# The last weight unit in sixteen transfers of eight partitions instead of one of 128

## The reference

```python
def moe_swiglu(h, w_router, w_gate, w_up, w_down):
    logits = (h @ w_router).astype(jnp.float32)
    top_vals, top_idx = lax.top_k(logits, TOP_K)
    top_w = jax.nn.softmax(top_vals, axis=-1)
    combine = jnp.sum(jax.nn.one_hot(top_idx, N_EXPERTS, dtype=jnp.float32) * top_w[..., None], axis=-2)
    y = jnp.zeros_like(h)
    for e in range(N_EXPERTS):
        y = y + combine[..., e:e + 1] * swiglu(h, w_gate[e], w_up[e], w_down[e])
    return y
# x = x + moe_swiglu(rms_norm(x, g_ffn_norm), ...); return rms_norm(x, g_final)
```

## Time and profile before

| | |
|---|---|
| median of 3 runs | 1340.99 us |
| lowest and highest | 1340.85 and 1341.76 us |
| the profiled execution's own time | 1340.35 us |
| its span, from the first to the last instruction | 1338.6 us |
| mean granted clock of TensorE, share of full speed | 0.998 |
| mean rate of the DMA engines over the span | 332 GB/s |

### The profile page before, as it was taken

How to read it: one execution, slowest core, us unless ns; L and a number is a source line. 1 busy time by engine, 2 the same in 40 slices (tenths; PEclk the granted TensorE clock), 3 DMA queues, 4 the chain that set the end, 5 groups by cost and what they waited for, 6 DMA issues and landing times.

```text
span 1338.6 us, 20750 instructions
## 1 busy us (share of the span) xinstructions
PE 1315.4 (98%) x8608; PEld 712.9 (53%) x8608; DVE 677.1 (51%) x1352; ACT 458.1 (34%) x773; POOL 3.6 (0%) x9
## 2 busy tenths in 40 slices
PE   9999999999999999999999999999999999999977
PEld 8887888888888778333333333333333333333322
DVE  5768765554767775444333553342533443433533
ACT  6565554443556554312121212112212112112112
POOL 0000000000000000000000000000000000000000
PEclk9999999999999999999999999999999999999999
DMA  9743555545575369999999999999999999999995
GB/s 350 272 142 99 188 186 189 189 157 160 187 259 188 111 252 364 394 426 426 426 428 426 426 429 425 427 427 427 427 424 429 426 426 429 426 427 426 428 426 207
DMA packets 68387, 444.46 MB, mean 332 GB/s; under 512 B 4632, under 2 KB 10280, under 8 KB 46656
## 3 DMA queue, kind: packets, MB, share of 16 engines
q1 hardware_dynamic: 66688, 440.36, 81.7%
q10 hardware_dynamic: 1296, 2.12, 0.6%
q0 software_dynamic: 304, 0.60, 0.1%
HBM read 442.01 MB, written 1.05 MB: 331 GB/s over the span
## 4 chain that ended last, share of the span: by engine, by line
PE 85%; DMA 6%; DVE 4%; ACT 2%; issue 1%; SPq 0%; DVEq 0%; ACTq 0%
PE A L543 22%; PE A L538 11%; PE DN L543 11%; PE A L532 7%; PE A L534 7%; PE A L533 7%; DMA pair<-in_moe_w_in 6%; PE DN L538 5%; PE T L2196 2%; PE DN L534 2%; PE DN L532 2%; PE DN L533 2%; DMA xs<-in_x 1%; PE A L1957 1%; PE T L534 1%
## 5 line engine op out<-in xcount | busy, mean ns | idle before, releaser
L543 PE MATMUL A<-pair,heTf 128*32 128x512 f32 x2688 | 295.3, 592 | 0.0
L507 DVE TENSOR_TENSOR parts<-raw,parts 128x2048 fp32r<-128x2048 f32 (+3 forms) x83 | 180.0, 2174 | 97.7 <-ACT parts L500 97.6
L538 PE MATMUL A<-pair,heTf 128*64 128x512 f32 x448 | 199.3, 594 | 7.1 <-DMA pair<-in_moe_w_in 7.1
L539 PE MATMUL A<-pair,heTf 128*64 128x512 f32 x448 | 199.4, 594 | 0.0
L543 PEld LDWEIGHTS A<-pair,heTf 128*32 128x32 f32 x2688 | 86.1, 110 | 197.4 <-issue 197.4
L500 ACT ACTIVATE parts<-raw 128x2048 fp32r<-128x2048 f32 (+3 forms) x83 | 150.9, 1821 | 106.3 <-PE A L534 56.4
L1649 DVE STREAM_TRANSPOSE aTf<-one_av 32x128 f32<-32x128 f32 x560 | 169.1, 302 | 12.9
L532 PE MATMUL A<-parts,hTh 128*128 128x512 f32 (+2 forms) x432 | 167.7, 388 | 0.8 <-DVE parts L507 0.6
L533 PE MATMUL A<-parts,hTh 128*128 128x512 f32 (+2 forms) x432 | 163.6, 379 | 0.0
L534 PE MATMUL A<-parts,hTl 128*128 128x512 f32 (+2 forms) x432 | 163.6, 379 | 0.0
L543 PE MATMUL DN<-pair,aTf 128*32 128x512 f32 x1344 | 149.5, 593 | 0.0
(11 more groups left out here) (355 smaller groups left out, 1422.5 us busy)
## 6 DMA issues: line engine op xcount, KB each, us to landing
pair<-in_moe_w_in SPq DMA_DIRECT2D x112, 2048.0 KB, 33.7
pair<-in_moe_w_down SPq DMA_DIRECT2D x55, 2048.0 KB, 33.5
raw<-in_w_in SPq DMA_DIRECT2D x22, 1024.0 KB, 6.0
raw<-in_dense_w_down SPq DMA_DIRECT2D x11, 1024.0 KB, 5.0
raw<-in_dense_w_gate SPq DMA_DIRECT2D x10, 1024.0 KB, 5.1
raw<-in_dense_w_up SPq DMA_DIRECT2D x10, 1024.0 KB, 5.1
raw<-in_w_out SPq DMA_DIRECT2D x8, 1024.0 KB, 5.3
raw<-in_w_br_mla SPq DMA_DIRECT2D x4, 1024.0 KB, 5.1
```

The source lines that it names most:

```text
L507: nc.vector.tensor_tensor(lo[:, :n], raw_of(u)[:, :n], hi[:, :n].bitcast(F32), ALU.subtract).then_inc(lo_done, 1)
L538: nc.tensor.matmul(o[:SMALL], even, w_even, start=start, stop=stop)
L539: return nc.tensor.matmul(o[SMALL:], odd, w_odd, start=start, stop=stop)
L543: return nc.tensor.matmul(o[at * QUARTER:(at + 1) * QUARTER], tokens, w, start=start, stop=stop, tile_position=(0, at * QUARTER))
```

## The change

The last unit is no longer issued as one transfer. A loop over the partitions issues sixteen, each for eight neighbouring partitions with 8 KB each. All add 16 to the same semaphore, so the count that PE waits for goes from 16 to 16 * 16 = 256. Source, destination, place in the issue order and everything else stay as they are.

```diff
             if u == LAST_UNIT:
-                return 16
+                return 16 * (P // 8)
...
                     sp.dma_start(pairs[pair][:, 0, :], src[:, :UNIT]).then_inc(pair_landed[pair], 16)
-                    sp.dma_start(pairs[pair][:, 1, :], src[:, UNIT:]).then_inc(last_landed, 16)
+                    for p in range(0, P, 8):
+                        sp.dma_start(pairs[pair][p:p + 8, 1, :], src[p:p + 8, UNIT:]).then_inc(last_landed, 16)
```

## The result

The changed kernel takes 1344.0 us (median of 14 runs, 1343.56 to 1344.73) against 1340.9 us for the kernel before on the same chip (14 runs, 1340.53 to 1341.76): a ratio of 1.0022, 95% interval 1.0014 to 1.0029. That is +3.1 us, with an interval of 1.9 to 3.9. The profiled execution has 1343.88 us and a span of 1342.1 us (before 1340.35 and 1338.6); its granted clock is 0.998.

What follows compares the result with a forecast made beforehand. The end was taken to hang on a weight pair landed at 1309.00, then compute, leaving the last unit 2.1 us of slack. Profiled 1340.35 + 3.0 = 1343.35 us, stated as 1344.0 against the median; range 1340.8 to 1348.9.

Steps and rivals of the forecast that it cites:

- What bounds the end, and the slack: At the end, the last unit's landing is off the chain, with 2.1 us of slack before PE needs it.
- Packets: In the last unit's transfers, eight engines carry sixteen rows each: 4.95 us in place of 2.47.
- Rival D: One engine carries all rows of the last unit: 39.6 us, +35 us, 1376; chance 0.01.
- Issue: Fifteen more issues on SP, 0.51 us each unhindered or 3.89 if held; taken as no cost, +1.3 us at worst.
- Completions: In the small transfers each engine posts one after every row, not every eighth; taken as nothing, 7.5 us at most.
- Rival C: Each completion of the small transfers is waited out: +8.0 us, 1349.0; chance 0.04.
- Where these rows start: A laggard engine starts the last unit's rows at 1321.2; at full pace PE starts 0.5 us later.
- wrong if the chain up to 1324 moves: The prediction's own failure sign: nothing in its sum touches the chain before PE takes the last activations.
- The pace of these rows: Neighbouring partitions slow the last unit's rows by a factor of 1.5: 7.4 us, landing 1328.6, PE +3.0 us.
- A: Rival, hidden: eight engines at full pace on the last unit, +0.5 us, 1341.5; chance 0.33.
- B: Rival, in step: four engines share one's pace on the last unit, 19.8 us, PE +15.3 us, 1356.3; chance 0.04.
- Chances: For the whole kernel: slower 0.46, within 0.2% (2.7 us) 0.51, faster 0.03; the forecast itself 0.55.

Runs made afterwards that it cites:

- e9: e1 with the rows for partitions 64 and up written to the lower half of another buffer; 1341.02 us, ratio 1.0003.
- e2: Changed kernel with eight transfers of 16 neighbouring partitions in place of sixteen of eight; 1341.79 us, ratio 1.0006.
- e3: Changed kernel, but SP waits until the last pair's first half has landed before issuing the sixteen transfers; 1351.66 us, ratio 1.0080.
- e1: Changed kernel with each of the sixteen transfers taking eight partitions four apart; 1342.97 us, ratio 1.0016.
- e8: e1 with partitions 64 to 127 first and 0 to 63 after; 1343.95 us, ratio 1.0022.
- e6: e3 with weights read from rows four apart, still written into neighbouring partitions; 1350.61 us, ratio 1.0072.
- e4: e3 with the eight partitions of each transfer four apart, read and written; 1353.98 us, ratio 1.0097.
- e7: e3 with neighbouring weight rows read into partitions four apart; 1353.76 us in its only run.

## Why the prediction was right or wrong

*What bounds the end, and the slack.* Right. The sum from the changed kernel's own landings: the first half lands 3.3 us later (1324.5 for 1321.2), the last unit 1329.1 - 1324.5 = 4.6 us after it where it was 2.4, so 2.2 us from the doubled rows; 3.3 + 2.2 - 2.1 of slack = 3.4 us, and PE is 3.39 us late. e9 and e2 show the slack swallowing each part, or nearly.

*Packets.* Right: eight engines, by the 112 new packets and by the share of 0.51 in e3. Rival D is out. *Issue* and *Completions.* Right: e9 has them all at +0.03 us. Rival C is out. The issues took 1.04 us each beside the full queue, between the two ends that were weighed.

*Where these rows start* is the step that failed. The prediction let the laggard be done with the first half at 1321.2, as before, and wrote that nothing in its sum touches the chain up to 1324. But the leading engines reach the small transfers at about 1312, 8 us ahead (before, they stopped at about 1314, and their eight rows of the last unit take 2.47 us), while the lagging ones are still on the pair of group 5 and on the first half. Their crowded rows bring the pace down to 17.0 GB/s an engine (e3 takes the crowding away from that stretch and the first half is in after 42.4 us; e9 keeps the leading engines out of the others' partitions and it is in after 42.3). The start moved by 3.3 us. By the prediction's own test, "wrong if the chain up to 1324 moves", this part is wrong.

*The pace of these rows* was mis-sized for the place where it was used: a factor of 1.5 on all sixteen rows of the laggard, 7.4 us. Where the laggard does them, alone with two or three others, the pace is 25.7 GB/s, a factor of 1.03, and the rows take some 5 us. A factor of about 1.5 was there (26.5 / 17.0 = 1.56), but earlier and on other transfers' rows. That 7.4 us from 1321.2 and the 7.9 us measured from there to 1329.1 nearly agree is chance: two errors, a start 3.3 us too early and a run 2.8 us too long (7.4 for the 4.6 between the landings), cancel but for 0.5.

*Rivals.* A (hidden, +0.5 us) had the right pace for the last rows and missed the same thing: the time before them. What A describes is e9. B (in step, factor four) was seen nowhere; eight engines all at it, in e3, have 1.9, and not all of that from neighbours. *Chances.* +3.1 us is a little over the bound of 2.7 us and its interval reaches to both sides, so the cases meant for slower and for no change can't be told apart by the time alone.

What stays open: why, with neighbours written, every engine's rows stretch from 1312 on, those of the lagging engines too, though strided writes to the same lower partitions hardly slow anybody (23.9 GB/s an engine in e1 until 1316). What the neighbours as such cost in the full queue is open too: e8 writes none and loses 2.96 us, e1 2.10, and the intervals of both overlap with that of the change (1.9 to 3.9). That the lagging engines write the upper half was read from e1, e8 and e9, and not from the engines' numbers.

## What to carry to other kernels

When a transfer is cut into pieces, ask what the engines that reach the pieces first do to the transfers *ahead* in the queue: with engines 8 us apart, the pieces run beside the tail of the others, and a busy DMA share at an unchanged total rate (14 engines moving what nine did) is the sign. Divide GB/s by busy engines window by window before and after, for every window in which the new rows can run, not only where they end. And count a slack once: two costs that each fit into it can together be seen in full.

## What was not expected of the hardware

- With nothing else in the queue, engines that write eight neighbouring partitions moved 14.1 GB/s each (e3; 13.7 in e6, which reads from rows four apart), and 19.2 with partitions four apart (e4); in the full queue it was 26.5.
- Rows four apart ran at 23.9 GB/s an engine in the lower half of the partitions and at 13.75 in the upper half, in which the lagging engines wrote; in the other order (e8) the slow stretch came first.
- Issuing a transfer to partitions four apart took SP 0.65 us where one to neighbouring partitions took 0.28 (e4 and e7 against e3).
- In e8 an idle stretch of 2.61 us before 1322.11 was followed by a granted clock of 0.50; in the changed kernel 2.46 us before 1321.54 left it at 1.00.
